# Router logits taken from the output projection's blocks, 1 MB expert loads, and unused products in three waits of the routing

## What is computed

```python
yl  = m @ w_out                                            # (512, 2048)
xl  = xl + mod_l[2] * yl
hl2 = rmsnorm(xl, norm2_w) * (1 + mod_l[4]) + mod_l[3]
scores = sigmoid(hl2 @ w_router)                           # 16 experts, 4 groups
# the best group of each token by its two best (scores + bias), and in it the two best experts
gate = gate / sum(gate)                                    # two weights per token
# rows sorted by expert into blocks of 128
yb = (silu(x_blk @ w1[e]) * (x_blk @ w3[e])) @ w2[e]       # w1, w3: 2048x512, w2: 512x2048
f  = sum over a token's two experts of gate * yb
out = rmsnorm(xl + mod_l[5] * f, final_norm_w)
```

## Time and profile before

| | |
|---|---|
| median of three runs | 2496.8 us |
| the profiled execution's own time | 2496.68 us |
| its span in the trace | 2495.1 us |
| TensorE busy | 2221.1 us, 89% of the span |
| VectorE, ScalarE, GpSimd busy | 1586.5, 980.4 and 610.5 us |
| moved by DMA | 532.11 MB, a mean of 213 GB/s |
| granted TensorE clock, mean | 0.95 of full speed |

### The profile page before, as it was taken

How to read it: one execution, slowest core, us unless ns; L and a number is a source line. 1 busy time by engine, 2 the same in 40 slices (tenths; PEclk the granted TensorE clock), 3 DMA queues, 4 the chain that set the end, 5 groups by cost and what they waited for, 6 DMA issues and landing times.

```text
span 2495.1 us, 34704 instructions
## 1 busy us (share of the span) xinstructions
PE 2221.1 (89%) x10837; PEld 1815.6 (73%) x10837; DVE 1586.5 (64%) x1886; ACT 980.4 (39%) x1186; POOL 610.5 (24%) x698
## 2 busy tenths in 40 slices
PE   2679999999999998999999998986699999999990
PEld 1169888888888885877777876775677777777770
DVE  2076645666566564765666665335479999989984
ACT  3044422333233333222222222222167777777771
POOL 0025514543445343111111111001002122121222
PEclk9889999999999999999999998998589999999995
DMA  9945422222222223667777766441589999999985
GB/s 373 417 132 167 145 85 81 84 81 77 81 86 78 84 75 94 219 214 225 226 224 236 231 193 237 146 125 47 189 300 366 392 367 379 383 379 378 384 328 219
DMA packets 386603, 532.11 MB, mean 213 GB/s; under 512 B 15072, under 2 KB 261344, under 8 KB 379008
## 3 DMA queue, kind: packets, MB, share of 16 engines
q1 hardware_dynamic: 353216, 392.93, 46.0%
q0 software_dynamic: 33344, 138.63, 15.9%
HBM read 494.77 MB, written 36.73 MB: 213 GB/s over the span
## 4 chain that ended last, share of the span: by engine, by line
PE 72%; DVE 6%; issue 4%; DMA 2%; ACT 2%; POOL 1%; ACTq 0%; SPq 0%; POOLq 0%; DVEq 0%
PE ps L624 12%; PE ps L626 12%; PE ps L625 12%; PE ps L888 5%; PE ps L890 5%; PE ps L889 5%; DVE e_lo L1790 3%; PE ps L795 2%; PE ps L838 2%; PE ps L839 2%; PE ps L796 2%; PE ps L797 2%; PE ps L840 2%; PE ps L684 2%; DMA e_raw<-in_w_e 1%
## 5 line engine op out<-in xcount | busy, mean ns | idle before, releaser
L1362 DVE TENSOR_TENSOR w_lo<-raw,w_hi 128x1024 fp32r<-128x1024 f32 x272 | 351.2, 1292 | 413.3 <-ACT w_hi L1006 413.1
L1790 DVE TENSOR_TENSOR e_lo<-e_raw,e_hi 128x1024 fp32r<-128x1024 f32 x384 | 500.6, 1326 | 64.0 <-ACT e_hi L1233 52.4
L1006 ACT CAST w_hi<-raw 128x1024 fp32r<-128x1024 f32 x272 | 284.6, 1047 | 643.9 <-PE ps L626 321.8
L624 PE MATMUL ps<-hl_hi,w_hi 128*128 128x512 f32 x1280 | 509.2, 398 | 0.5 <-DVE s_ctx L1435 0.5
L626 PE MATMUL ps<-hl_hi,w_lo 128*128 128x512 f32 x1280 | 499.3, 390 | 0.0
L625 PE MATMUL ps<-hl_lo,w_hi 128*128 128x512 f32 x1280 | 499.2, 390 | 0.0
L1233 ACT CAST e_hi<-e_raw 128x1024 fp32r<-128x1024 f32 x384 | 400.1, 1057 | 166.9 <-PE ps L890 117.6
L626 PEld LDWEIGHTS ps<-hl_hi,w_lo 128*128 128x128 f32 x1280 | 240.9, 188 | 50.9
L624 PEld LDWEIGHTS ps<-hl_hi,w_hi 128*128 128x128 f32 x1280 | 241.2, 188 | 49.8 <-issue 1.7
L625 PEld LDWEIGHTS ps<-hl_lo,w_hi 128*128 128x128 f32 x1280 | 241.2, 188 | 49.1 <-issue 1.7
L888 PE MATMUL ps<-e_hi,xe_hi 128*128 128x512 f32 x512 | 207.8, 406 | 35.5 <-DVE e_lo L1790 32.6
(11 more groups left out here) (323 smaller groups left out, 3561.5 us busy)
## 6 DMA issues: line engine op xcount, KB each, us to landing
e_raw<-in_w_e SPq DMA_DIRECT2D x384, 512.0 KB, 7.1
raw<-in_w_in SPq DMA_DIRECT2D x208, 512.0 KB, 3.7
ada<-in_w_ada POOLq DMA_DIRECT2D x64, 1024.0 KB, 5.9
ada_ring<-in_w_ada SPq DMA_DIRECT2D x16, 2048.0 KB, 17.0
raw<-in_w_out SPq DMA_DIRECT2D x32, 512.0 KB, 4.8
block_outputs<-y_sb POOLq DMA_DIRECT2D x32, 512.0 KB
raw<-in_w_branch_pool SPq DMA_DIRECT2D x16, 512.0 KB, 3.9
raw<-in_w_branch_hgrn SPq DMA_DIRECT2D x16, 512.0 KB, 4.0
```

The lines of the kernel that those rows point to most:

```text
L624: mm(dst, hi, rhs_hi[:, k, :], start=(k == 0), stop=False)
L1006: act_e.copy(w_hi[:, hslot, :], raw[:, slot, :]).then_inc(hi_done, 1)
L1362: tt(w_lo[:, hslot, :], raw[:, slot, :], w_hi[:, hslot, :].bitcast(F32), ALU.subtract).then_inc(split_done, 1)
L1790: tt(e_lo[:, hslot, :], e_raw[:, slot, :], e_hi[:, hslot, :].bitcast(F32), ALU.subtract).then_inc(e_split, 1)
```

## The change

- **w_out stage.** TensorE signals after each token tile of a block's last unit (`w_mm`), so that VectorE empties bank by bank. ScalarE's sums of squares of a block move behind the next block's first high part. x2, not h2, is transposed (`turn_x2`, 4 transposes per tile and block, in the next block after units 1 and 2) and multiplied with w_router scaled by the columns of m4 (`part_logits`, after unit 4, four fp32 products of 32 x 512 in four column groups of the array, summed over the blocks in one bank). VectorE also multiplies x2 with the block's m4 (`modulated`) and prepares the scaled router weights (`columns`). Two DMAs read m4 and m3 as columns, one number at a time (`m34_col`).
- **Logits.** Copy of that bank, four products with `group_sum` that add the four column groups and turn the result, times the inverse root, plus the share of m3 (`m3_logit`, from one small product before block 3). The whole rows h2 are finished by one VectorE pass per tile (`normed`), in the places that the listing shows, and stored by GpSimd.
- **Routing.** The counting and table products run on one-pass operands, the counts in five products in place of 28 passes; `e_lo_unit(0, 0)` stands before `table_i`. `keep_busy(n)` issues n products of 128 x 512 whose result nobody reads: 28 before the wait for `sel_rdy`, 24 before that for the one-hot slots, 8 before and 24 after that for `table_rdy`.
- **Expert stage.** A load is 1 MB, 8 KB in one piece per partition, into 6 places; 6 places for split parts and `AHEAD` = 5. The weights' rows are dealt to partitions in another order, so the transposes read x and the activation with a stride of 16 and of 4 numbers. The first expert's loads and first high parts no longer wait for the table. Six loads are started by the time of the first gather. GpSimd no longer multiplies with m5. In the gap between experts 0 and 1 the next units' parts come after the transposes.
- **End.** ScalarE scales y0 by its gate (`y0_rdy`); VectorE makes four passes per tile in place of three.

```diff
@@ expert weights: 8 KB in one piece per partition @@
-    w_e1_d = w_e1[0].rearrange("e (k p) n -> e p k n", p=P)
+    w_e1_d = w_e1[0].rearrange("e (p k) n -> e p k n", p=P)
...
@@ SyncE @@
-            sp.wait_ge(h2_rdy, NTOK - 1)
-            sp.wait_ge(h2_last, 1)
-            for q in range(16):
-                load_e(q, q % 8, w13(w_e1_d if q < 8 else w_e3_d, 0, q % 8))
+            for n in range(8):
+                if n == 2:
+                    sp.wait_ge(x2_rdy, 20)
+                if n == 3:
+                    sp.wait_ge(part_mm, 4)
+                if n == 4:
+                    sp.wait_ge(h2_rdy, NTOK)
+                if n == 5:
+                    sp.wait_ge(y_out, 16 * NTOK)
+                if n == 6:
+                    sp.wait_ge(xe_in, 16)
+                load_e(n, n % EP, piece(0, n))
...
@@ TensorE, w_out and routing @@
+            def part_logits(cb):
+                pe.wait_ge(x2T_rdy, X2T + cb * 4 + 4)
+                pe.wait_ge(ws_rdy, cb + 1)
+                for j in range(4):
+                    last = mm(ps[32 * j:32 * j + 32, 6, :], w_scaled[:, j, :], x2T[:, j, :], start=(cb == 0),
+                              stop=(cb == 3), tile_position=(0, 32 * j))
+                last.then_inc(part_mm, 1)
...
+                        if u == 7 and t < NTOK - 1:
+                            last.then_inc(w_mm, 1)
                     last.then_inc(units_done, 1)
+                    if cb and u in (1, 2):
+                        turn_x2(cb - 1, 2 * u - 2)
+                        turn_x2(cb - 1, 2 * u - 1)
+                    if cb and u == 4:
+                        part_logits(cb - 1)
...
+            keep_busy(28)
             pe.wait_ge(sel_rdy, 1)
...
+            keep_busy(24)
             pe.wait_ge(onehot_rdy, 1)
...
+            keep_busy(8)
             pe.wait_ge(table_rdy, 1)
+            keep_busy(24)
...
@@ VectorE @@
+            normed(0)
+            dve.wait_ge(lg_step, LG_MM)
+            step(tt(R3(3), ps[:, 0, 0:NTOK * E].rearrange("p (t e) -> p t e", e=E),
+                    stat2[:, 3, :].unsqueeze(2).to_broadcast([P, NTOK, E]), ALU.mult))
+            dve.wait_ge(m3_step, 2)
+            tt(R3(3), R3(3), m3_logit[:].unsqueeze(1).to_broadcast([P, NTOK, E]), ALU.add).then_inc(lg_step, 1)
...
+            normed(1)
+            dve.wait_ge(lg_step, LG_SCORE)
...
+            normed(2)
+            normed(3)
             dve.wait_ge(pos_mm, 1)
...
+            e_lo_unit(0, 0)
             dve.wait_ge(tab_mm, 1)
...
@@ end, VectorE @@
-                step(stt(out=o, in0=y0[:, i, :], scalar=gate_w[:, 0, i:i + 1], in1=x2[:, i, :], op0=ALU.mult,
+                dve.wait_ge(y0_rdy, i + 1)
+                step(stt(out=o, in0=y1[:, i, :], scalar=gate_w[:, 1, i:i + 1], in1=y0[:, i, :], op0=ALU.mult,
                          op1=ALU.add))
-                stt(out=o, in0=y1[:, i, :], scalar=gate_w[:, 1, i:i + 1], in1=o, op0=ALU.mult, op1=ALU.add
-                    ).then_inc(f_sum, 1)
+                step(tt(o, o, m5_row[:], ALU.mult))
+                tt(o, o, x2[:, i, :], ALU.add).then_inc(f_sum, 1)
...
@@ GpSimd @@
+            for i, at in ((0, 2 * D), (1, D)):
+                pool.dma_start(m34_col[:, i, :], mod_d[0, at:at + D].rearrange("(k p) -> p k", p=P),
+                               allow_slow_non_contiguous=True).then_inc(rows_in, 16)
...
                     pool.wait_ge(y_ev, b * 4 + (6 + 2 * n))
-                    own.did(tt(y_sb[:, cols], y_sb[:, cols], m5_row[:, cols], ALU.mult))
-                    own.wait()
                     pool.dma_start(y_d[ds(b * BLK, BLK), cols], y_sb[:, cols]).then_inc(y_out, 16)
```

More of the change, by code:

```diff
@@ L866, in _ @@
-            logits(NTOK - 1)
-            pe.wait_ge(sel_rdy, 1)
-            chosen = rt[:, 8, :].rearrange("p (t e) -> p t e", e=E)
-            for t in range(NTOK):
-                for s in range(t + 1):
-                    mm(ps[:, 1, t * E:(t + 1) * E], upper[:] if s == t else ones[:], chosen[:, s, :],
-                       start=(s == 0), stop=(s == t))
-            for s in range(NTOK):
-                last = mm(ps[:, 2, 0:E], ones[:], chosen[:, s, :], start=(s == 0), stop=(s == NTOK - 1))
+            project(1)
@@ new lines, in _ @@
+            project(2)
+            pe.wait_ge(col_rdy, COL_SUM)
+            pe.wait_ge(x2T_rdy, X2T + 8)
+            mm(bank(TR, E), ones[:], m3_part[:], start=True, stop=True).then_inc(m3_step, 1)
+            project(3)
+            for t in range(NTOK):
+                turn_x2(3, t)
+            part_logits(3)
+            pe.wait_ge(lg_step, LG_PART)
+            pe.wait_ge(col_rdy, COL_GROUPS)
+            pe.wait_ge(w_ev, 20)
+            for t in range(NTOK):
+                last = mm(ps[:, 0, t * E:(t + 1) * E], osq[:, t * P:(t + 1) * P], group_sum[:], start=True, stop=True)
@@ new lines, in _, with keep_busy @@
+            last.then_inc(lg_step, 1)
+            pe.wait_ge(col_rdy, COL_EXACT)
+            def keep_busy(n):
+                for _ in range(n):
+                    mm(bank(UB), upper_r[:], m_hi[:, 8, :], start=True, stop=True)
+            keep_busy(28)
+            pe.wait_ge(sel_rdy, 1)
+            counts = ps[:, 1, 0:(NTOK + 1) * E]
+            chosen = chosen_r[:].rearrange("p t e -> p (t e)")
+            mm(counts, upper_r[:], chosen, start=True, stop=False, skip_group_check=True)
@@ L875, in _ @@
+            for s in range(1, NTOK + 1):
+                last = mm(counts[:, s * E:], ones_r[:], chosen[:, 0:(NTOK + 1 - s) * E], start=False,
+                          stop=(s == NTOK), skip_group_check=True)
             last.then_inc(pos_mm, 1)
+            keep_busy(24)
             pe.wait_ge(onehot_rdy, 1)
             for n in range(2 * NTOK):
-                last = mm(ps[:, 3, 0:NBLK], slot_1[:, n, :], block_tok[:, n, :], start=(n == 0),
+                last = mm(ps[:, 3, 0:NBLK + 1], slot_1[:, n, :], block_tok_r[:, n, :], start=(n == 0),
@@ L1300, in _ @@
                             act_hi(b + E)
-                    y_copy(b + E, b * 24 + (E * 24 + 28))
+                    y_copy(b + E, b * 24 + (E * 24 + EH + 24))
                 act_e.nop()
+            for i in range(NTOK):
+                act_e.wait_ge(y_in[i], 32)
+                activate(y0[:, i, :], y0[:, i, :], ACT.Copy, scale=gate_w[:, 0, i:i + 1]).then_inc(y0_rdy, 1)
             for i in range(NTOK):
@@ L1815, in act_lo @@
                    actT_hi[:].rearrange("p k t -> p (k t)").bitcast(F32), ALU.subtract).then_inc(actT_rdy, 1)
-            AHEAD = 3
-            for q in range(AHEAD):
-                e_lo_unit(q, q, q)
+            AHEAD = EH - 1
+            for q in range(1, AHEAD):
+                e_lo_unit(q, q)
             for part in range(4):
@@ L1823, in _ @@
                 n = q + AHEAD
[L1824 removed]
+                if n < 16:
+                    e_lo_unit(n, n)
                 if q == 8:
                     silu(0, True)
[L1827 removed]
+            gate_up(0, EH + 16, True)
             for part in range(4):
                 x_lo(1, part)
+            for n in range(AHEAD):
+                e_lo_unit(16 + n, 16 + n)
             with dve.Fori(1, E) as e:
@@ L2087, in _ @@
             with pool.Fori(1, E) as e:
-                own.loop(e - 1, 4)
+                own.loop(e - 1, 2)
                 pool.wait_ge(xe_in, e * 16 + 16)
@@ L2099, in _ @@
                 with pool.If(b < n_extra):
-                    own.loop(b, 4)
+                    own.loop(b, 2)
                     pool.wait_ge(xe_T, b * 4 + 4 * (E + 1))
```

426 lines of the change are left out of this document (233 added, 193 removed).

## The result

The changed kernel takes 2411.5 us (median of 4 runs, 2407.7 to 2413.5) against 2495.1 us (4 runs, 2489.6 to 2497.2): a ratio of 0.967, 95% interval 0.9645 to 0.9688, so 83.6 us less. The forecast was 2423 with a range of 2400 to 2455. The profiled execution of after had 2407.73 us, its span is 2406.1; it was the fastest of the four, so a sum by stages comes to 89 us where the medians give 84.

A forecast was written before the change was run, and what follows sets the result against it. It took TensorE (89% busy), with DMA also near its limit in the expert loop, and chains in routing as bounds. Terms +1.7 - 42.7 - 2.5 - 0.9 + 0.4 - 36 + 6.5 = -73.5 on 2496.68 gave 2423 us, range 2400 to 2455.

The forecast's parts named there:

- the loop: Fifteen turns of the expert loop: each goes from 38.6 to 36.2 us, -36 us; bounds -52 and -9.
- the w_out stage: w_out stage: 8.9 us of waits removed, transposes 5.5, `part_logits` 3.8 and `m34_col` 1.3 added; +1.7 us.
- the end: Final stage: GpSimd's two passes go, -4.7; ScalarE's scaling adds 2.0, VectorE's fourth passes 9.2; +6.5 us.
- the way from the table to the first product: Gather and transposes before the first expert product: 13.6 us becomes 11.1, 1.2 off each of two parts; -2.5 us.
- Routing: From the last w_out product to the table: 79.2 us becomes 36.5, count and table products hidden under other steps; -42.7 us.
- after, six loads are long in by then, so the gather has the DMA engines to itself: Table to first product: the gather no longer shares DMA with the first expert's loads; 1.2 us off.
- The rival of unused products on the path: Before the first transposes and into the ranks' end, half-clock unused products add 5 us: 2428; chance 0.05.
- all waits gone, stride free: Rival for the expert loop: TensorE's own 35.1 us a turn, 2407 us in total; chance 0.13.
- the forecast's 1.1 us for the stride: Expert loop: strided weight loads for 20 transposes a turn, +60 ns each, cost TensorE 1.1 us (0 to 2.8).
- Limit (c): Expert loop: the stall after `y_copy` goes, with five units of lead, 6.8 us against 2.6 needed, and GpSimd's L2078 gone.
- Limit (b): Expert loop, DMA: larger packets raise 380 GB/s to 421, so a turn's 14.7 MB take 35.0 us instead of 38.6.
- The wait in the loop: Expert loop after `y_copy`: VectorE's next four e_lo take 7.61 us, 1.9 each, against 1.33 when GpSimd is silent.

The follow-up runs named there:

- the control: The changed kernel itself, unaltered, run again as the base on the chip of the kernels beside it: 2411.8 us (2408.7 to 2413.1).
- the short lead alone: Changed kernel with four places for split parts instead of six, so three units ahead of the products: 2414.7 us, ratio 0.967.
- the multiply alone: Changed kernel with GpSimd's m5_row multiply back before each store of y, and without ScalarE's scaling of y0: 2427.2 us, ratio 0.972.
- both together: Changed kernel with GpSimd's multiply back and four places for split parts; 1 MB loads and 8 KB runs stay: 2446.7 us, ratio 0.980.

## Why the prediction was right, point by point

The sum had the right size, 73.5 us less against 89 in the profiles and 84 in the medians. Three terms were off by more than 3 us: the loop, 14 too cautious, the w_out stage, 3.3 too cautious, and the end, 3.5 too kind. Most errors were too cautious; the end and the way from the table to the first product (2.4) go the other way, so little of the sum's fit comes from errors that cancel.

- **Routing** (-42.7 predicted, -45.1 measured): right in mechanism and nearly in size. `part_logits` took 1.07 us (1.3), the small products 1.06 (1.2), `sel_rdy` came 17.8 us behind the last product (19.2), since ScalarE's pairs ended at 4.4 instead of 5.3 and the ranks took 7.2 instead of 7.4. The counts were free, as said.
- **w_out stage** (+1.7, -1.6): the 8.9 us of waits went. Transposes and `part_logits` added 7.3, not 9.3 (by difference), and VectorE never waited for `m34_col`, which I had given 1.3. The two columns landed 14.4 to 15.0 us after their issue, longer than the 11.4 of the row that I had taken, and 2.9 us before the need: here the price was wrong and the distance right.
- **Table to the first product** (-2.5, -0.1): the step that failed is "after, six loads are long in by then, so the gather has the DMA engines to itself". The DMA engines' share in this stretch was 0.94, against 0.56 before. The sixth load waits for the stored rows of h2 and starts less than 0.5 us before the table (at 1750.34 in the run with the earlier index, whose table came at 1750.80), so it is under way beside the gather, and two loads of rows of 1 MB are issued behind it. But the sharing was worth less than I took: from issue to landing the gather took 6.5 us before and after, and 5.9 in the run with the norm on ScalarE and GpSimd, where the sixth load (issued at 1757.11, 4.9 us to landing) had landed before the gather's issue at 1765.23. So having the DMA engines to itself gives it 0.6 us at most, not 1.2. What grew is the way to its issue. GpSimd's index copy took 0.95 us instead of 0.19, because four e_lo now stand on VectorE at that moment; it ended at 1753.56, just as the first of them did (1752.29 + 1.22). The rounds of transposes gained 1.0 (4.9 us), the gather's way from the table lost 0.9 (8.6 us). The rival of unused products on the path is at the edge here (0.49 us of wait behind them) and real once the gather is issued earlier.
- **Loop** (36.2 us a turn predicted, 35.2 measured): the rival "all waits gone, stride free" had the turn, 35.1; the forecast's 1.1 us for the stride was mis-sized, it is 0.08. The load is longer by 53 ns (193 against 140), near the +60 taken from the moving operand, but nearly all of it is hidden. By the Trainium skill (SBUF — State Buffer, section "Door 1: The DMA port swizzle") a read that goes to a new 16-byte line each time pays, which both strides do; the durations of 193 and 204 ns agree with it, the turn hardly feels it. Limit (c) was right: the stall went, worth 45.9 of the 49.6 us of fourteen turns. Limit (b) was wrong in its premise: 380 GB/s at a share of 1.02 was read as what the packets allow, and in loads of 1 MB they allow 399. Packets and load size gave 4 of these 50 us by themselves; with the stall gone the packets keep 19 that would else be lost.
- **The wait in the loop** was put as "VectorE's next four e_lo take 1.9 each". That was a mean: VectorE is stopped for the length of GpSimd's pass. The Trainium skill (SBUF — State Buffer, section "SBUF: two separate sides") says that a VectorE instruction with two SBUF inputs and a GpSimd instruction take their shared port as an exclusive lock for the whole instruction. The four steps of 4.37 to 4.94 us agree, and so does the 6.47 us pass in the trace of before.
- **End** (+6.5, +10.0): copy to first pass was right (-2.7 predicted, -2.8 measured). The passes took 43.3 us instead of 39.7: I counted VectorE's work and left out that ScalarE, in program order, does all four scalings, each waiting for its gather, before the first square, and then loads a table (1.28 us). Reordering it gave those 4 us back.
- **Not predicted**: the last block's 2.4 us, some 1.6 of which are this execution's luck. It ran at a clock of 1.00, where it had 0.90 before; but in the control's profile of the same program it ran at 0.89 and took as long as before (16.15 us between the y copies, against 16.13). What decides it, no run tells.

## What to carry to other kernels

Between two engines that block one another, count the blocked time as the whole length of the other's pass, and ask whether the blocked engine has the slack to catch up: over fourteen turns the short lead alone cost 2.1 us, the multiply alone 26.4 and both together 45.9. Don't read a limit off a DMA share near 1 or off the rate beside it; look for waits on loads, and change the bytes or the packets to be sure. Before work goes to another engine, look in the trace at hand for a place where the two already run side by side. When an engine gets new work at the end, follow its program order past the sum of its busy time, and when a cover (here the unused products) is sized to a wait, size it again after the wait is shortened.

## What was not expected of the hardware

- Beside a GpSimd pass of 4.5 us over SBUF a VectorE step of 12 to 64 numbers a partition, else 0.2 us, took 4.4 to 4.9 us; other steps in the gaps kept their 0.2 us. The other way round, a GpSimd copy of one number a partition took 0.95 us instead of 0.19 and ended with VectorE's pass.
- With six loads of 1 MB in flight, 8 KB runs gave 419 GB/s without being the limit, and 2 KB runs 399 to 401 while being it.
- Strided weight loads of 193 ns instead of 140, twenty in a turn, cost 0.08 us a turn.
- The first gather of 128 rows took 5.9 to 6.5 us from issue to landing in every profile, with no load beside it (5.9) or one to three; in the loop, with six loads in flight, the median was 11.1.
- TensorE's granted clock from 1766 to 1772 us was 1.00 in one execution of the changed kernel and 0.72 in another of the same program, with the same instructions ahead; the first y copy moved by 1.3 us with it (79.0 against 80.3 us behind the table). The last block's clock was 1.00 and 0.89 in the same two.
